# A hybrid decoder layer: the q, k, v units over the first token chunk alone, samples first, and the input norm's weight inside the hi/lo split

## The chip, the cores and the metric

The kernel is one program on one core of a Trainium2 chip. The metric is the device time of one execution in microseconds (us), as the median of several runs. Engines are named as in the profile: PE is TensorE's matmul stream and PEld its weight loads, DVE is VectorE, ACT is ScalarE, POOL is GpSimd, and SP (SyncE) issues most DMAs. Each engine works through its own instructions in order and waits on semaphores.

## The reference

One inference step of one layer, over 1024 prompt tokens and 8 samples of 4 tokens each (1056 tokens in all), model width 1024, everything in f32:

```
h = rmsnorm(x, g_mix_norm);  z = h @ w_in            # 2304 columns: q 512, k 128, v 128, B 512, C 512, h 512
q, k = rope(rmsnorm(q)), rope(rmsnorm(k))            # 8 q heads, 2 kv heads, width 64
o_attn = sliding-window (128) attention with a sink per head      # samples: over a cache of 128 keys
o_conv = B * conv3(C * h)                            # depthwise, causal
x = x + concat(rmsnorm(o_attn), rmsnorm(o_conv)) @ w_o
x = x + relu(rmsnorm(x) @ w_up)^2 @ w_down           # 4096 wide
x = x + sigmoid(rmsnorm(x) @ w_ple_gate) * (p @ w_ple)
```

## The kernel before, in words

The tokens lie on the free axis in three chunks of 352 (`CH`), the prompt first and the 32 sample tokens last. Every matrix product is made in three passes: each operand is split into a rounded part (`_hi`) and the rest (`_lo`), and PE multiplies hi by hi, lo by hi and hi by lo. For one unit of 128 output columns and one chunk that is a *fill*: 8 slices of the contraction times 3 passes, 24 matmuls of 128x352 into one of three `acc` banks (function `fill`). A fill needs its unit's weights split, which is ACT's `split_hi` and then `split_lo` on DVE or POOL, and then sends SP for the weights that take the freed slot; `w_st`, `w_hi` and `w_lo` have two slots each.

The input projection has 18 units, 54 fills with the index g: units 0 to 5 are q, k and v (`U_CONV` = 6), the others are C, h and B for four slices of the short convolution. Fill g is unit g // 3, chunk g % 3. A function `plan_inproj` gives the steps of attention that each engine does behind fill g (`at[g]`). For a tile t (0 the samples, 1 to 8 the prompt's blocks of 128) these are: B turns q, k, v to tokens on partitions (PE) and squares them; E norms and rotates (DVE, POOL's half of the sine term, ACT's and DVE's hi/lo split into `st_q`, `st_k`); S turns them back; Q makes the scores, DVE's masked maxima (`prob`), ACT's exponentials; D the denominators (POOL); P and R turn the probabilities; V and W multiply by v, ACT moves half of the result (`cross`), DVE adds and scales (`o_tok`); W also has ACT's square and POOL's root for the norm; N scales by it (ACT); O turns the result back. `plan_aux` hands these steps four of the five `aux` banks in turn, the fifth to V, W and O.

Ahead of the fills, x comes in 12 tiles of 88 rows: DVE squares (`x_sq`), POOL takes the root, ACT scales a copy (`x_nrm`), PE turns it, DVE multiplies by the norm's weight into `h_tmp`, ACT rounds (`act_hi`), POOL subtracts (`act_lo`). PE turns ten tiles (`ahead = 6` beyond the first four) before fill 0.

Behind fill 53 the output projection has 8 units of 3 fills (`out_units`). Each also turns a column slice of x (`x_col`, one buffer, loaded by SP once `x_turned` says that the last one was read) for the residual. A chunk of its input is ready when ACT and POOL have split attention's part (`mix_attention`, `lo_of_attention`) and DVE has normed the convolution's (`norm_conv`, `mix_conv`). The MLP and the embedding gate follow.

Of the kernel before, what the change touches and what calls it, by code (L numbers as in the profile page):

```python
# [25 lines left out]
P = 128  # L26
# [40 lines left out]
def plan_inproj():  # L67
# [44 lines left out]
def plan_aux(at):  # L112
# [3 lines left out]
    names = [("vec", 0, 0)]  # L116
    for g in range(3 * U_OUT):
        if g < NCH:
            names += [("x", g * XPC + t, h) for t in range(XPC) for h in range(2)]
        if g == NCH:  # L120
            names.append(("vec", 1, 0))
        if g > 3 * U_OUT - NCH:
# [17 lines left out]
def hybrid_step(nc, ins, outs):  # L140
# [49 lines left out]
    w_lo = place("w_lo", [P, 2, D], F32R)  # L190
    sq_sum = place("sq_sum", [P, NT], F32)
# [10 lines left out]
    kc = place("kc", [P, 4, DEC_B, WIN], F32R, conv_at)  # L202
    u_p = place("u_p", [P, SEQ + 2], F32)
# [4 lines left out]
    h_tmp = place("h_tmp", [P, 2, 4, XT], F32)  # L208
    root_c = place("root_c", [P, 2, CH], F32, cursor[0] - 4 * 2 * CH)
    x_at = cursor[0]  # L210
    tok = place("tok", [P, QK + KW], F32)
    ropea = place("ropea", [P, QK], F32)
    ropeb = place("ropeb", [P, QK], F32)
    st_q = place("st_q", [P, NQ, P], F32R)
    st_k = place("st_k", [P, 4, P], F32R)
    qt = place("qt", [P, NQ * P], F32R)
    kt = place("kt", [P, 2, 4 * P], F32R)
    v_parts = place("v_parts", [P, 3, NKV, 2, HD], F32R)
    x_end = cursor[0]
# [12 lines left out]
    columns = {"ms": NX, "rs": NX, "mse": NX, "mx": NQ, "nm": NQ, "sn": NQ, "es": NQ, "l": NQ, "den0": NQ, "den1": NQ,  # L232
# [1642 lines left out]
```

## Time and profile before

| | us |
|---|---|
| median of 3 runs (1413.68 to 1415.95) | 1413.86 |
| the profiled execution, first to last instruction (its span) | 1409.7 |
| of it, before the first fill of the input projection | 41.15 |
| fills 0 to 8 | 41.15 to 82.17 |
| fills 9 to 52 and most of attention | 82.17 to 388.61 |
| fill 53 and unit 0 of the output projection | 388.61 to 426.65 |
| units 1 to 7 of the output projection | 426.65 to 537.29 |
| the norm, MLP and gate, to the end | 537.29 to 1409.7 |

The times are ends of groups of matmuls in the trace. The profiled execution is known by its span; the runs' median lies 4.2 us above it, and times for the runs are worked out by carrying that distance along.

### The profile page before, as it was taken

Reading aid. Unit: us, or ns where it says so; the run is one execution under the profiler, and the core shown is the slowest. Engines: PE = TensorE matmul, PEld = TensorE weight load, DVE = VectorE, ACT = ScalarE, POOL = GpSimd, SP = SyncE. Lnnn points to the kernel's source line nnn. Section 1 sums busy time; section 2 is a strip of 40 time slices with the busy share of each in tenths; the row PEclk is TensorE's granted clock in tenths of the full one; section 3 lists DMA queues with packets and bytes.
Section 4 is the critical chain, followed back from the end, with each engine's and each line's share of the span. In section 5 each row is a group of like instructions: output and inputs, shape, how many; then the busy total and the mean of one; then the engine's idle time right before and its main releaser. Section 6 shows DMA issues by size and latency. Waiting matters only on the chain.

```text
span 1409.7 us, 21751 instructions
## 1 busy us (share of the span) xinstructions
PE 1315.8 (93%) x8348; PEld 1298.5 (92%) x8348; DVE 716.3 (51%) x1271; ACT 401.9 (29%) x801; POOL 199.2 (14%) x216
## 2 busy tenths in 40 slices
PE   3899988997958889999999999999999999999997
PEld 2899877897958889999999999999999999999997
DVE  6302757677575446435445344354453544587342
ACT  5332445455434222102111011121110211254232
POOL 6623434434130000000000000000000000041000
PEclk9999999999989899999999999999999999999999
DMA  5521011001103221321111111111111111111221
GB/s 153 131 60 32 1 48 30 16 16 35 46 17 75 62 65 41 77 52 45 48 47 54 45 45 45 45 45 45 45 45 45 45 50 39 46 45 54 69 68 46
DMA packets 111132, 70.99 MB, mean 50 GB/s; under 512 B 3226, under 2 KB 109622, under 8 KB 111064
## 3 DMA queue, kind: packets, MB, share of 16 engines
q1 hardware_dynamic: 110584, 68.37, 17.7%
q0 software_dynamic: 480, 1.93, 0.5%
q8 instruction: 33, 0.54, 0.2%
q14 instruction: 19, 0.16, 0.0%
q10 hardware_dynamic: 16, 0.00, 0.0%
HBM read 65.69 MB, written 5.54 MB: 51 GB/s over the span
## 4 chain that ended last, share of the span: by engine, by line
PE 77%; DVE 8%; ACT 4%; issue 4%; DMA 3%; POOL 2%; SPq 1%; DVEq 0%; ACTq 0%
PE acc L1534 71%; PE aux L1549 3%; DMA x_col<-in_x_sample 2%; DVE prob L1265 2%; PE aux L1534 1%; POOL act_lo L669 1%; DVE conv L1365 1%; POOL sq_sum L793 1%; DMA w_st<-in_w_in 1%; PE aux L1682 1%; DVE ropea L1218 1%; DVE o_tok L1305 1%; ACT sq_new L1097 1%; DVE pt_lo L1281 1%; ACT w_hi L805 0%
## 5 line engine op out<-in xcount | busy, mean ns | idle before, releaser
L1534 PE MATMUL acc<-xg_hi,w_hi 128*128 128x352 f32 x960 | 312.0, 325 | 0.0
L1534 PE MATMUL acc<-xg_lo,w_hi 128*128 128x352 f32 x960 | 307.8, 321 | 0.0
L1534 PE MATMUL acc<-xg_hi,w_lo 128*128 128x352 f32 x960 | 307.7, 321 | 0.0
L1534 PE MATMUL acc<-a_hi,w_hi 128*128 128x352 f32 x768 | 247.7, 323 | 0.0
L1534 PE MATMUL acc<-a_lo,w_hi 128*128 128x352 f32 x768 | 246.1, 320 | 0.0
L1534 PE MATMUL acc<-a_hi,w_lo 128*128 128x352 f32 x768 | 245.9, 320 | 0.0
L1534 PE MATMUL acc<-act_hi,w_hi 128*128 128x352 f32 x624 | 215.1, 345 | 13.2 <-issue 12.8
L1534 PE MATMUL acc<-act_hi,w_lo 128*128 128x352 f32 x624 | 208.3, 334 | 0.0
L1534 PE MATMUL acc<-act_lo,w_hi 128*128 128x352 f32 x624 | 208.2, 334 | 0.0
L1449 DVE TENSOR_TENSOR xt<-acc,xt 128x352 f32<-128x352 f32 x192 | 100.3, 522 | 179.1 <-PE acc L1534 178.1
L805 ACT ACTIVATE w_hi<-w_st 128x1024 fp32r<-128x1024 f32 x98 | 102.9, 1050 | 280.0 <-PE acc L1534 273.8
L1534 PEld LDWEIGHTS acc<-xg_lo,w_hi 128*128 128x128 f32 x960 | 180.5, 188 | 0.2
L1534 PEld LDWEIGHTS acc<-xg_hi,w_hi 128*128 128x128 f32 x960 | 180.1, 188 | 0.3 <-issue 0.2
L1534 PEld LDWEIGHTS acc<-xg_hi,w_lo 128*128 128x128 f32 x960 | 180.0, 188 | 0.0
L1534 PEld LDWEIGHTS acc<-a_lo,w_hi 128*128 128x128 f32 x768 | 144.3, 188 | 0.0
L1534 PEld LDWEIGHTS acc<-a_hi,w_hi 128*128 128x128 f32 x768 | 144.1, 188 | 0.0
L1534 PEld LDWEIGHTS acc<-a_hi,w_lo 128*128 128x128 f32 x768 | 143.9, 187 | 0.0
L793 POOL TENSOR_TENSOR sq_sum<-sq_sum,sq_new 128x352 f32<-128x352 f32 x24 | 23.2, 966 | 837.8 <-ACT sq_new L1097 837.8
L1534 PEld LDWEIGHTS acc<-act_hi,w_hi 128*128 128x128 f32 x624 | 124.8, 200 | 14.2 <-issue 13.2
L1068 ACT ACTIVATE a_hi<-relu 128x352 fp32r<-128x352 f32 x96 | 47.9, 499 | 292.6 <-DVE relu L1432 292.6
L1432 DVE SCALAR_TENSOR_TENSOR relu<-acc,rstd 128x352 f32<-128x352 f32 x96 | 50.3, 524 | 154.5 <-PE acc L1534 154.5
L1534 PEld LDWEIGHTS acc<-act_lo,w_hi 128*128 128x128 f32 x624 | 124.7, 200 | 0.0
(199 smaller groups left out, 1598.6 us busy)
## 6 DMA issues: line engine op xcount, KB each, us to landing
w_st<-in_w_up SPq DMA_DIRECT2D x32, 512.0 KB, 4.1
w_st<-in_w_down SPq DMA_DIRECT2D x32, 512.0 KB, 3.4
w_st<-in_w_in SPq DMA_DIRECT2D x18, 512.0 KB, 3.9
w_st<-in_w_o SPq DMA_DIRECT2D x8, 512.0 KB, 4.6
w_st<-in_w_ple_gate SPq DMA_DIRECT2D x8, 512.0 KB, 4.3
x_nat<-in_x_prompt SPq DMA_DIRECT2D x11, 352.0 KB
x_col<-in_x_prompt SPq DMA_DIRECT2D x8, 484.0 KB
out<-y_col SPq DMA_DIRECT2D x8, 484.0 KB
```

The costliest lines, as they stand in the source:

```text
L669: pool.tensor_tensor(act_lo[:, 4 * h:4 * h + 4, cols], h_tmp[:, h, :, :], act_hi[:, 4 * h:4 * h + 4, cols], ALU.subtract).then_inc(h_lo, 1)
L793: pool.tensor_tensor(sq_sum[:, chunk(c)], sq_sum[:, chunk(c)], sq_new[:, :], ALU.add)\
L805: act.activation(w_hi[:, s, :], w_st[:, s, :], ACT.Copy).then_inc(whi_ready, 1)
L1068: act.activation(a_hi[:, m, chunk(c)], relu[:, f % 2, :], ACT.Square).then_inc(a_hi_ready, 1)
L1097: act.activation(sq_new[:, :], xt[:, 2 * m + n2, chunk(c)], ACT.Square).then_inc(squared, 1)
L1218: dve.tensor_tensor(heads(ropea, m), qn, cos[:, None, :].broadcast_to([m, NQ + NKV, HD]), ALU.mult).then_inc(cos_ready, 1)
L1265: e = dve.tensor_tensor_reduce(prob[:, h * 2 * P:(h + 1) * 2 * P] .rearrange("p (s k) -> p s k", s=2), bank[:, cols].rearrange("p (s k) -> ...
L1281: frees(dve.tensor_tensor(pt_lo[0:rows_, cols], bank[0:rows_, 0:width], pt_hi[0:rows_, cols], ALU.subtract), step, t, i)
L1432: dve.scalar_tensor_tensor(out=relu[:, f % 2, :], in0=acc[c][:, 0:CH], scalar=0.0, in1=rstd[:, chunk(c)], op0=ALU.max, op1=ALU.mult)\
L1449: dve.tensor_tensor(xt[:, n, chunk(c)], acc[f % 3][:, 0:CH], xt[:, n, chunk(c)], ALU.add)\
L1534: ins_ = pe.matmul(out, w[a][cols], x[b][tile_], start=(k == 0 and p == 0), stop=(k == len(terms) - 1 and p == 2))
L1549: ins_ = pe.transpose(out[dst], src, ident[0:src.shape[0], 0:src.shape[0]])
```

## The change

It leaves every matmul of the products as it is and orders the first stage anew.

- Tokens are numbered with the samples first. `plan_fills` lists the 54 fills: units 0 to 5 over chunk 0; then units 4 and 5 over chunks 1 and 2, while their weights still stand; then units 0 to 3 over chunks 1 and 2, for which four weight blocks are loaded a second time (`EXTRA` = 4); then the other units as before. `LAST_FILL` decides when a slot's next weights are split. DVE makes the lo part of loads 0 to 6, POOL of the rest.
- x is scaled in its own buffer and turned by chunk, 4 tiles of one slice of 128 columns at a time. ACT writes the hi part from the turned bank with the norm's weight as its scale, and DVE writes the lo part from the bank by one multiply-subtract. `h_tmp`, DVE's multiplication and POOL's subtraction go.
- The x tiles of chunks 1 and 2 are normed and turned behind fills 0 to 7 (`X_NORM_AT`, `X_TURN_AT`).
- Attention begins behind fill 7 and not 18. Tiles start at fills 7, 11, 14, 18, 22 and so on by four (before: 18, 22 and so on by three), in the order 1, 2, 0, 3 to 8. N and O come one fill later than before.
- Some tables, `smask`, the cached keys and values have other places and load times; the rotary table comes tile by tile from POOL.
- A unit of the output projection turns all three chunks of its x slice ahead of its first fill.

The core of the diff:

```diff
+ORDER = [1, 2, 0, 3, 4, 5, 6, 7, 8]
+POS = {t: n for n, t in enumerate(ORDER)}
...
+    fills = [(u, 0, u) for u in range(U_CONV)]
+    fills += [(u, c, u) for c in (1, 2) for u in (4, 5)]
+    fills += [(u, c, U_CONV + u) for u in range(4) for c in (1, 2)]
+    fills += [(u, c, u + EXTRA) for u in range(U_CONV, U_OUT) for c in range(NCH)]
...
+EXTRA = 4
+FILLS = plan_fills()
+LAST_FILL = {load: g for g, (u, c, load) in enumerate(FILLS)}
...
+SPLIT_AT = {g: [n + 2 for n in LAST_FILL if LAST_FILL[n] == g] for g in range(3 * U_OUT)}
+
+X_NORM_AT = {0: [4], 1: [5], 2: [6], 3: [7], 4: [8], 5: [9, 10], 6: [11]}
+X_SQUARE_AT = {-1: [4], 0: [5], 1: [6], 2: [7], 3: [8], 4: [9, 10], 5: [11]}
+X_TURN_AT = {3: [(1, k) for k in range(4)], 4: [(1, k) for k in range(4, 8)],
+             6: [(2, k) for k in range(4)], 7: [(2, k) for k in range(4, 8)]}
+AHEAD = 4
...
-        at[3 + b].append(("k", b))
-        at[4 + b].append(("K", b))
-    at[12].append(("C", 0))
-    starts = [18, 22, 25, 28, 31, 34, 37, 40, 43]
-    for t, g in enumerate(starts):
+        at[CACHE_AT + b // 2].append(("k", b))
+        at[CACHE_AT + 1 + b // 2].append(("K", b))
+    at[CACHE_AT].append(("C", 0))
+    starts = [7, 11, 14, 18, 22, 26, 30, 34, 38]
+    for t, g in zip(ORDER, starts):
         late = 1 if t == 0 else 0
         for step, off in (("B", 0), ("E", 1), ("S", 3), ("Q", 4), ("D", 4), ("P", 6), ("V", 7), ("R", 7), ("W", 8),
-                          ("N", 9 + late), ("O", 9 + late)):
+                          ("N", 10 + late), ("O", 10 + late)):
             at[g + off].append((step, t))
...
             for t in range(XPC):
                 load_x(t)
-            load_w(0, in_unit(0), None)
-            for t in range(XPC, 2 * XPC):
-                load_x(t)
-            load_w(1, in_unit(1), None)
-            for t in range(2 * XPC, NX):
+            load(0)
+            load(1)
+            load_x(4)
+            load(2)
+            load_x(5)
+            load_x(6)
+            load(3)
+            load_x(7)
+            load(4)
+            filled(sp, "x", 0, KT - 1)
+            load_x(8)
+            load(5)
+            for t in range(9, NX):
                 load_x(t)
...
+            def norm_x(t):
+                act.wait_ge(x_rs, t + 1)
+                act.activation(x_tile(t)[0:XT, :], x_tile(t)[0:XT, :], ACT.Copy,
+                               scale=stat["xrs"][0:XT, t:t + 1]).then_inc(x_normed, 1)
+
+            def hi_of_x(c, k):
...
+                bank = filled(act, "x", c, k)
+                act.activation(act_hi[:, k, chunk(c)], bank[:, 0:CH], ACT.Copy,
+                               scale=vec[:, V_MIX + k:V_MIX + k + 1]).then_inc(h_hi, 1)
...
+            def lo_of_h(c, k):
+                bank = filled(dve, "x", c, k)
+                dve.wait_ge(h_hi, KT * c + k + 1)
+                frees(dve.scalar_tensor_tensor(out=act_lo[:, k, chunk(c)], in0=bank[:, 0:CH],
+                                               scalar=vec[:, V_MIX + k:V_MIX + k + 1], in1=act_hi[:, k, chunk(c)],
+                                               op0=ALU.mult, op1=ALU.subtract), "x", c, k)
...
+            for g, (u, c, n) in enumerate(FILLS):
+                if g == FIRST_FILL[n]:
+                    pe.wait_ge(wlo_ready, n + 1)
+                if g >= NACC:
+                    pe.wait_ge(acc_free[g % NACC], g // NACC)
+                fresh = g in (0, U_CONV, U_CONV + 2)
+                fill(c, n % 2, act_in, g % NACC, lo_of_h_ready(c) if fresh else None)
...
+                for c_, k in X_TURN_AT.get(g, []):
+                    turn_x(c_, k)
...
             def out_units(i, first):
                 for s in range(2):
-                    pe.wait_ge(wlo_ready, 2 * i + (U_OUT + s + 1))
                     pe.wait_ge(xcol_landed, 96 * i + 48 * (s + 1))
                     for c in range(NCH):
                         pe.wait_ge(aux_free[c], 2 * i + (OUT_USE[c] + s))
                         turn(aux[c], [((every, slice(k * XT, (k + 1) * XT)), x_col[0:XT, XPC * c + k, :])
                                       for k in range(XPC)]).then_inc(x_turned, 1)
+                    pe.wait_ge(wlo_ready, 2 * i + (W_OUT + s + 1))
+                    for c in range(NCH):
                         pe.wait_ge(att_lo, c + 1)
                         pe.wait_ge(mix_lo, c + 1)
```

Three places show how instructions stand on an engine. The first is the start of PE's stream; `aux<-ident,x_nrm` is a turn of x. Before:

```order
L1549 MATMUL aux<-ident,vec_nat 128x8
L1549 MATMUL aux<-ident,x_nrm 128x88 x80
L1534 MATMUL acc<-act_hi,w_hi 128x352
L1534 MATMUL acc<-act_lo,w_hi 128x352
L1534 MATMUL acc<-act_hi,w_lo 128x352
```

and of the change:

```order
L1633 MATMUL aux<-ident,vec_nat 128x8
L1633 MATMUL aux<-ident,x_nat_94 128x88 x20
L1618 MATMUL acc<-act_hi,w_hi 128x352
L1618 MATMUL acc<-act_lo,w_hi 128x352
L1618 MATMUL acc<-act_hi,w_lo 128x352
L1633 MATMUL aux<-ident,x_nat_94 128x88 x4
L1618 MATMUL acc<-act_hi,w_hi 128x352
```

The first fill moved from behind 80 turns (ten tiles) to behind 20, and the rest of its chunk's turns went in between its matmuls.

The second is ACT in the middle of attention, from the exponentials of one tile (`prob`) on; `st_q`, `st_k` are step E of the next tile, `cross` and `aux,stats<-o_tok` step W, `o_tok<-o_tok` step N, `pt_hi` step P. Before:

```order
L913 ACTIVATE prob,stats<-prob,stats 128x256 x8
L918 ACTIVATE stats<-stats 128x8
L878 ACTIVATE st_q<-ropea 128x8x64
L880 ACTIVATE st_k<-ropea 128x256
L805 ACTIVATE w_hi<-w_st 128x1024
L935 ACTIVATE cross<-aux 128x256
L943 ACTIVATE aux,stats<-o_tok 128x512
L888 ACTIVATE v_parts<-tok 128x2x64
L895 ACTIVATE qt<-aux 128x512 x2
L900 ACTIVATE kt<-aux 128x512
```

and of the change:

```order
L978 ACTIVATE prob,stats<-prob,stats 128x256 x8
L983 ACTIVATE stats<-stats 128x8
L1000 ACTIVATE cross<-aux 128x256
L1008 ACTIVATE aux,stats<-o_tok 128x512
L943 ACTIVATE st_q<-ropea 128x8x64
L945 ACTIVATE st_k<-ropea 128x256
L871 ACTIVATE w_hi<-w_st 128x1024
L1080 ACTIVATE conv<-u_p,vec 128x1024
L1081 ACTIVATE conv<-u_s,vec 128x32
L1012 ACTIVATE o_tok<-o_tok,stats 128x512
L992 ACTIVATE pt_hi<-aux 128x512 x2
```

Step W moved ahead of step E, and the copies of step S (`qt`, `kt`) moved behind N and P.

The third is PE at the start of the output projection. Before:

```order
L1549 MATMUL aux<-ident,tail 18x128 x4
L1549 MATMUL aux<-ident,x_col 128x88 x4
L1534 MATMUL acc<-act_hi,w_hi 128x352
...
L1534 MATMUL acc<-act_hi,w_lo 128x352
L1695 MATMUL aux<-sq_sum,ones 128x352
L1549 MATMUL aux<-ident,x_col 128x88 x4
```

and of the change:

```order
L1633 MATMUL aux<-ident,tail 18x128 x4
L1633 MATMUL aux<-ident,x_col 128x88 x12
L1618 MATMUL acc<-act_hi,w_hi 128x352
```

The turns of chunks 1 and 2 moved from between the fills to ahead of them.

## Rows read from the trace of the kernel before

**Rows 1.** Busy time by stretch: PE, PEld, DVE, ACT, POOL, granted clock, DMA share, GB/s.
```profile
0.00:41.15 41.15, 14.04 (x81) 11.85 (x82) 29.02 (x42) 21.52 (x30) 26.73 (x37) 1.00 0.62 160
41.15:82.17 41.02, 40.54 (x253) 39.97 (x253) 8.51 (x15) 14.92 (x30) 20.36 (x30) 1.00 0.37 96
82.17:388.61 306.44, 277.47 (x1850) 269.87 (x1849) 178.33 (x387) 139.87 (x364) 115.03 (x115) 0.96 0.11 31
388.61:426.65 38.04, 22.92 (x127) 21.26 (x126) 30.26 (x38) 15.08 (x22) 13.84 (x11) 0.87 0.12 30
426.65:537.29 110.64, 96.47 (x588) 94.52 (x587) 50.76 (x93) 35.21 (x72) 0.00 (x0) 0.92 0.27 63
```

**Rows 2.** Waits of PE from 82.17 to 388.61: total, times, longest us.
```profile
PE aux L1549 <- ACT qt L895: 21.6, 7, 6.3
```

**Rows 3.** Timeline of the opening: start, us, DVE, ACT, POOL and PE.
```profile
11.56 1.21 DVE L1150 CUSTOM_DVE_ANT_0 x_sq<-x_nat 88x1024 f32<-88x1024 f32 x1
14.99 1.22 DVE L501 TENSOR_TENSOR w_lo<-w_st,w_hi 128x1024 fp32r<-128x1024 f32 x1
19.41 2.83 DVE L1150 CUSTOM_DVE_ANT_0 x_sq<-x_nat 88x1024 f32<-88x1024 f32 x1
12.77 1.06 ACT L805 ACTIVATE w_hi<-w_st 128x1024 fp32r<-128x1024 f32 x1 [0.59 <-DMA w_st<-in_w_in]
13.73 1.13 ACT L826 ACTIVATE x_nrm<-x_nat,stats 88x1024 f32<-88x1024 f32 x1
51.86 1.00 ACT L982 ACTIVATE qkv<-acc 128x352 f32<-128x352 f32 x2
14.41 0.55 POOL L657 TENSOR_TENSOR stats<-stats,half 88x1 f32<-88x1 f32 x1
40.00 1.44 PE L1549 MATMUL aux<-ident,x_nrm 88*128 88x88 f32 x8 [3.33 <-ACT x_nrm L826]
```

**Rows 4.** Page, costliest groups: xcount, then busy us, mean ns.
```profile
L1432 DVE SCALAR_TENSOR_TENSOR relu<-acc,rstd 128x352 f32<-128x352 f32 x96 | 50.3, 524 | 154.5 <-PE acc L1534 154.5
```

**Rows 5.** Groups by form, 218.43 to 349.96 (five tiles): busy us, mean ns.
```profile
L913 ACT ACTIVATE prob<-prob,stats 128x256 f32<-128x256 f32 x40 | 19.8, 496 | 15.1 <-DVE stats L1273 15.1
L1297 DVE TENSOR_TENSOR o_tok<-aux,cross 128x256 f32<-128x256 f32 x10 | 4.2, 422 | 11.3 <-PE aux L1549 7.4 <-ACT cross L935 3.9
L943 ACT ACTIVATE aux<-o_tok 128x512 f32<-128x512 f32 x5 | 3.0, 602 | 16.1 <-DVE o_tok L1305 16.1
L465 POOL TENSOR_TENSOR tok<-ropeb,rope_p 128x320 f32<-128x320 f32 x5 | 5.9, 1171 | 1.0 <-DVE ropeb L1212 0.9
L1222 DVE TENSOR_TENSOR ropea<-ropea,tok 128x640 f32<-128x640 f32 x5 | 4.1, 824 | 0.2
L878 ACT ACTIVATE st_q<-ropea 128x512 fp32r<-128x512 f32 x5 | 3.2, 634 | 6.0 <-DVE ropea L1222 6.0
L947 ACT ACTIVATE o_tok<-o_tok,stats 128x512 f32<-128x512 f32 x5 | 3.7, 731 | 0.0
L501 POOL TENSOR_TENSOR w_lo<-w_st,w_hi 128x1024 fp32r<-128x1024 f32 x5 | 13.0, 2600 | 8.4 <-ACT w_hi L805 8.4
```

**Rows 6.** Timeline of DVE around fill 53.
```profile
393.57 4.38 DVE L1320 SCALAR_TENSOR_TENSOR conv<-conv,vec,root_c 128x352 f32<-128x352 f32 x4
397.88 0.68 DVE L1309 TENSOR_TENSOR qkv<-aux,vec 128x512 f32<-128x512 f32 x1
406.81 2.65 DVE L1320 SCALAR_TENSOR_TENSOR conv<-conv,vec,root_c 128x352 f32<-128x352 f32 x4
```

**Rows 7.** The chain of work that ended last: start, us, what.
```profile
453.00 5.05 DMA x_col<-in_x_sample
458.69 5.43 PE acc L1534 x24
464.43 3.86 PE acc L1534 x24
...
540.02 641.01 PE acc L1534 x4032
```

More of the change, by code:

```diff
@@ L313, in hybrid_step @@
         tables_landed = sem("tables_landed")
+        rope_landed = [sem(f"rope_landed{s}") for s in range(2)]
         smask_landed = sem("smask_landed")
@@ L482, in pt_count, with exp_count @@
         def pt_count(t, step):
-            before = 0 if t == 0 else 6 + 4 * (t - 1)
+            before = sum(6 if x == 0 else 4 for x in ORDER[:POS[t]])
             return before + (0 if step == "P" else 3 if t == 0 else 2)
+        def exp_count(t):
+            return sum(NKV if x == 0 else NQ for x in ORDER[:POS[t]])
         def gains(at_, n, m):
@@ L923, in consume @@
                             filled(act, "V", t, "o")
-                        if i == 0 and step == "P" and t:
-                            filled(act, "W", t - 1, "o")
+                        if i == 0 and step == "P" and pos:
+                            filled(act, "W", before, "o")
                         rows_, width = (P, 4 * P) if i < 2 else (NS, P)
@@ L1153, in gain_h @@
-            def gain_h(t):
-                for h in range(2):
-                    bank = filled(dve, "x", t, h)
-                    if t >= 1:
-                        dve.wait_ge(h_lo, 2 * t - 1 + h)
-                    frees(dve.tensor_tensor(h_tmp[:, h, :, :], bank[:, 0:4 * XT].rearrange("p (k t) -> p k t", k=4),
-                                            gains(V_MIX + 4 * h, 4, XT), ALU.mult), "x", t, h)
+                dve.tensor_tensor_reduce(x_sq[0:XT, :], x_tile(t)[0:XT, :], x_tile(t)[0:XT, :], 1.0 / D, EPS,
+                                         ALU.mult, ALU.add, stat["xms"][0:XT, t:t + 1]).then_inc(x_ms, 1)
@@ L1173, in _ @@
                     split_lo(dve, 1, 2)
-            bank = filled(dve, "vec", 1, 0)
-            frees(dve.tensor_copy(vec[:, V_MLP:NV], bank[:, V_MLP:NV]), "vec", 1, 0)
-            done_with(dve, "vec", 1, 0)
+            for t in X_SQUARE_AT[-1]:
+                ms_of_x(t)
             def consume(step, t):
-                m = rows_of(t)
+                m, pos = rows_of(t), POS[t]
+                before = ORDER[pos - 1] if pos else None
                 w = NKV if t == 0 else NQ
@@ L1332, in _ @@
                 u, c = divmod(g, NCH)
+                for n in SPLIT_AT[g]:
+                    if n < DVE_SPLITS:
+                        split_lo(dve, n % 2, n + 1)
+                if g == VEC_AT:
+                    bank = filled(dve, "vec", 1, 0)
+                    frees(dve.tensor_copy(vec[:, V_MLP:NV], bank[:, V_MLP:NV]), "vec", 1, 0)
+                    done_with(dve, "vec", 1, 0)
+                for t in X_SQUARE_AT.get(g, []):
+                    ms_of_x(t)
+                for c_, k in X_TURN_AT.get(g, []):
+                    lo_of_h(c_, k)
                 if u >= U_CONV:
@@ L1528, in take_bank, with product @@
                 return aux[bank]
-            def product(out, w, x, terms, more=False):
+            def product(out, w, x, terms, before=None):
                 for k, (cols, tile_) in enumerate(terms):
+                    if before is not None:
+                        before(k)
                     for p, (a, b) in enumerate(((0, 0), (0, 1), (1, 0))):
```

529 lines of the change are left out of this document (273 added, 256 removed).

## The prediction

> **What bounds the kernel now.** I first read the busy time by stretch [rows 1]. PE is busy 14.04 of the first 41.15 us, 40.54 of the next 41.02, 277.47 of 306.44, 22.92 of 38.04 and 96.47 of 110.64; behind 540.02 the chain of waits is one piece of PE work, 641 us long [rows 7]. So PE sets the end, and what a change of order can win is the time for which PE stands still in the first 537 us: 27.1 us ahead of the first fill, 29.0 beside attention, 15.1 around fill 53, 14.2 in the output projection, and what a lower clock costs there (granted 0.87 and 0.92, against 1.00 at the start). The waits of PE name whom it waits for: of the 29.0 beside attention 21.6 are ACT's copy `qt`, seven times, the longest 6.3 [rows 2]. That is the end of a tile's way through E (DVE, POOL, ACT) and S (PE), for which before leaves two fills. In the output projection the chain goes through the load of `x_col`, 5.05 us, behind which the next fill takes 5.43 and the one after it 3.86 [rows 7].
>
> A fill is 3.86 us at full clock; with its split weights present and its banks free it has no other cost.
>
> **The opening.** Before the change PE turns ten x tiles and then begins. Each tile goes through a square (1.21 us, but 2.83 beside POOL), a root (0.55), the scaled copy (1.13) and PE's turns, 0.72 for four [rows 3]. With the change only four tiles stand ahead. 160 GB/s flowed in the first stretch [rows 1], and the weights' hi part begins at 12.77 [rows 3], when the same first tiles and weights have landed; so the fourth tile's copy is done by about 14.5, the hi part of its first bank at 15.6, two lo splits on DVE (1.22 and, for the bank, about 0.5) at 17.4. **The first fill starts at 17.5 and not at 41.15.** In it lie the turns of slices 4 to 7, which ACT and DVE answer in turn at about 0.5 each (ACT copies a chunk from a bank in 0.50 [rows 3]; for DVE's new multiply-subtract see below): it ends near 24. Fills 1 to 3 follow at 3.86 and end at 35.6. Then PE wants chunk 1 turned, and its last tile's norm waits in ACT's row behind a weight split (1.06) and two unit copies: 3.3 us, then eight banks at 0.35 to 0.5. Fill 4 ends at 44.3; fill 5, behind the rest of chunk 1, at 49.7; fill 6 at 53.5; the last tile of chunk 2 costs 1.6 more, and with the turns of chunk 2 and step B of the first tile fill 7 ends near 62.5 and **fill 8 at 66.8**, for 82.17 before: 15.4 won. Of the 23.6 won at the first fill, 8 go back to turns and norms that formerly lay ahead of it.
>
> The *new operation*, a multiply-subtract out of a PSUM bank, 24 times, has no row. Its nearest is DVE's relu, which has the same operands and size: 0.524 [rows 4], 12.6 us in all. From below nothing excludes that it hides wholly (it stands ahead of PE at fill 0 and at chunk changes only); from above, the square beside POOL shows a factor of 2.83/1.21 = 2.3 [rows 3], which would make it 29 us, of which a third, chunk 0's, is bare: +5. I take 0.52, as the POOL subtraction that stood beside it is gone. The Trainium skill (GPSIMD Engine Reference, section "8. Key points") says that GpSimd and VectorE share their way into SBUF and collide when VectorE runs in a two-port mode or reads two operands from SBUF. By that rule the new operation, with one operand in PSUM, is not slowed, and the sum stays as it is; by the squares' row taken for all operations it would be the 5 us more. No row shows this operation.
>
> **Fills 9 to 52 and attention.** PE's work in this stretch was 277.5 [rows 1]. Turns of the cached keys that before lay ahead of it come in (+2.1), step B of tile 1 goes out (0.85), step O of tile 8 comes in ahead of fill 53 (0.66): 279.4. Its waits I work out tile by tile. A tile now has four fills for a period and not three. Time is counted from the end of the fill behind which B stands. PE does B, Q and W (5.0), two fills and P (1.15) and comes to step O at 13.9. The row that must be through by then: the exponentials, eight at 0.50, end at 8.7, since the first wait for ACT's copies and DVE's square, sum and first maximum; then `cross` and two times DVE's addition 0.42 with its multiplication (10.15), ACT's square 0.60 and its read-out (11.0), POOL's root (12.0), and POOL's sine term of the *next* tile, 1.17 (13.2), DVE's addition 0.82 (14.05), ACT's `st_q` 0.63 with `st_k` (15.05) and only then step N, 0.73: 15.75 [rows 5]. W was moved ahead of E, but N stands behind E on ACT. **PE waits 1.85 in an undisturbed tile**, and this wait takes the place of the one for `qt`, which now has a fill more. Where POOL's weight split, 2.60 [rows 5], gets ahead of the sine term, up to 2.6 is added: the slot's last fill stands behind E of tiles 4 and 7 (fills 23 and 35), and a little later at fills 26 and 38 (1.5 to 2.5 for 5 and 8). Tile 4 also meets the samples' result on its way through memory (`o_moved`), for which ACT's row waits. So my waits are 9.1 for tiles 1, 2 and 0 together (the split parts of k, Q and S of the first tiles, which have no period to fill), 2.2 for tile 3, 7.1, 4.4, 1.85, 5.2 and 3.4 for tiles 4 to 8: **33.3, no less than the 29.0 of before**. Fill 52 ends at 66.8 + 279.4 + 33.3 = 379.5, for 388.61: **of 15.4, 9.1 are left.** The bounds: nothing of these waits, when N falls in time, and twice as much.
>
> **The tail.** At fill 53 DVE's four scalings of the convolution take 4.38 beside POOL's and step O's work, later 2.65, and step O takes 0.68 of DVE between them [rows 6]. Tile 8 is through long before, so both go: 1.73 + 0.68 = **2.4** (bounds 0 and 4). The chunks stay bound by DVE's and ACT's norm.
>
> **The output projection.** Its last seven units take 110.64 [rows 1], 15.8 each. Turned ahead, the slice frees `x_col` at the start of a unit, and its 5.05 us load [rows 7] has three fills, 11.6 us, to hide in; what follows at full clock is 3 fills of 3.86 and 12 turns, at half of the 0.18 that one took cold [rows 3] 1.0: 12.6 x 7 = 88.2. **22.4 won** (bounds 14 and 24: at the busy time with its slow stretches, 96.5 [rows 1], it would be only 14).
>
> The rest is untouched: four more loads keep the slots' order. The four loads themselves are hidden by fills 10 to 17, each 512 KB with two fills for it. **Sum: 9.1 + 2.4 + 22.4 = 33.9 off a span of 1409.7, 1375.8. The runs' median was 4.2 above the span, so 1380.**
>
> **The rivals.** *Four fills are enough.* If the split of a tile's work is less serial than I laid it (maxima and exponentials faster, POOL out of the way), PE waits 2 us and not 33.3: 1380 - 31 = 1349. For it: the waits of before have one name, `qt`, and the change gives just that one a third fill. Against it: N behind E, worked out above.
>
> *The loads pace the opening.* Fills 0 to 5 each need a new unit, with the x tiles of chunks 1 and 2 on the same queues. At the 160 GB/s of [rows 1] four units and five tiles (3.9 MB) take some 24 us, and the six fills with the turns 26 to 32. With little less bandwidth, or with slots freed too late (ACT's and DVE's splits stand behind norms), each fill waits one to two us: +7, 1387. By the Trainium skill (DMA: Bandwidth & Descriptors, section Specifications, Bandwidth) a core gets about 358 GB/s from HBM; by an estimate from that figure the first tiles and weights would land some 5 us earlier and the time would be about 1375. The rows of this kernel's own start, 160 GB/s, do not agree, and they decide.
>
> *The hoisted turn does not do what it says.* If the load's cost is not the wait but the slow fill behind it, or the load is late again (its issue stands behind other issues on SP), the 22.4 stay: 1402.
>
> *The other side.* Step order on ACT can turn the wait for N into a chain that is longer than four fills, so that every tile is late by the same amount. The gains, 33.9 with the waits at 33.3, are gone when the nine tiles wait 67.2 us, 7.5 each; beyond that it is slower; at 9 each, 81 us, the time would be 1380 + 48 = 1428. The longest wait before was 6.3 [rows 2], and the period has grown by a fill; little speaks for it.
>
> **How the numbers follow.** Forecast, 1366 to 1392: 0.50. Four fills enough, about 1349: 0.25. Loads pace the opening, about 1387: 0.14. Hoist without effect, about 1402: 0.05. The other side: 0.05, and 0.01 for the neighbourhood of no change. The first three hold 0.89; with some room for their edges the range is 1346 to 1398: from the waits all gone, and 3 us more, to the waits half as large again, or loads and new operation at their upper bounds. A measurement of this kernel can tell about 0.2% from no change, 2.8 us. Faster 0.93, the same 0.02, slower 0.05.
>
> **What would show it.** First fill at 17.5, with DVE's lo parts at 0.52 each; the end of fill 8 near 67, with no PE wait for a weight split; fill 52 at 379; PE waits of about 33 us between them, the most of them in step O for ACT's `o_tok` and behind it in S for `st_q`; output units 12.6 us apart, without `x_col` on the chain and with a clock near 1.00. Wrong it is if waits for weights or x stand in the first six fills, if PE's waits are far from 33, or if the units remain near 15.8.

## The result, and the profile after

The changed kernel takes 1406.85 us (median of 4, 1405.78 to 1407.92); the kernel before took 1414.9 beside it. The ratio is 0.9946, 95% interval 0.9927 to 0.9965: faster by 0.5%, some 8 us, where 34 were forecast. The profiled execution spans 1406.1 us, and the median lies 0.7 above it (4.2 before). In e8 and in e12 below one execution ran far slower than the others (1521.4 and 2699.3 us); their medians are those of the others.

Busy time of the changed kernel by stretch, cut at the same events as [rows 1] (first fill, fill 8, fill 52, unit 0 and unit 7 of the output projection; columns as there):

```profile
0.00:18.34 18.34, 3.39 (x22) 3.09 (x22) 7.52 (x13) 9.63 (x12) 5.69 (x19) 1.00 0.69 161
18.34:71.25 52.91, 48.36 (x302) 47.18 (x302) 28.50 (x46) 27.03 (x43) 10.57 (x22) 0.90 0.58 146
71.25:408.43 337.18, 290.19 (x1863) 283.00 (x1862) 176.43 (x395) 145.51 (x375) 117.29 (x125) 0.90 0.12 34
408.43:446.37 37.94, 24.86 (x121) 23.07 (x122) 29.46 (x33) 14.79 (x21) 12.88 (x10) 0.78 0.12 30
446.37:533.17 86.80, 86.80 (x589) 86.67 (x588) 50.59 (x92) 34.34 (x71) 0.00 (x0) 1.00 0.34 80
```

| stretch, us | before | after | moved | forecast |
|---|---|---|---|---|
| to the end of fill 8 | 82.17 | 71.25 | -10.9 | -15.4 |
| fills 9 to 52, attention | 306.44 | 337.18 | +30.7 | +6.3 |
| fill 53, unit 0 of the output projection | 38.04 | 37.94 | -0.1 | -2.4 |
| units 1 to 7 | 110.64 | 86.80 | -23.8 | -22.4 |

The rest, to the end, takes 872.93 for 872.41. So one of the four terms came about as worked out (units 1 to 7), the opening brought some 70% of what was forecast, the tail nothing, and attention's stretch swallowed it all: it has 47.0 us of PE standing still (337.18 less 290.19) for 29.0, and 12.7 more of PE busy, at a granted clock of 0.90 for 0.96. PE's waits in it (total, times, longest), where [rows 2] had `qt`:

```profile
PE aux L1633 <- ACT o_tok L1012: 29.5, 8, 8.2
PE aux L1677 <- DVE st_k L1299: 8.3, 2, 4.3
PE aux L1657 <- DVE k_parts L1255: 2.6, 1, 2.6
...
PE aux L1633 <- ACT qt L960: 1.3, 1, 1.3
```

The wait for `qt` is gone and one for `o_tok` (step N) stands in its place, larger. ACT's timeline shows why, here in a period in which PE stood ready for step O of tile 4 from 269.84 to 276.00 (`prob` is tile 5, `st_q` and `st_k` are tile 6; start, us):

```profile
265.42 0.49 ACT L978 ACTIVATE prob<-prob,stats 128x256 f32<-128x256 f32 x1
...
267.39 0.60 ACT L1008 ACTIVATE aux<-o_tok 128x512 f32<-128x512 f32 x1 [1.02 <-DVE o_tok L1376]
...
271.51 0.63 ACT L943 ACTIVATE st_q<-ropea 128x512 fp32r<-128x512 f32 x1 [3.40 <-DVE ropea L1293]
272.04 0.40 ACT L945 ACTIVATE st_k<-ropea 128x256 fp32r<-128x256 f32 x1
272.35 1.04 ACT L871 ACTIVATE w_hi<-w_st 128x1024 fp32r<-128x1024 f32 x1
273.97 1.15 ACT L1080 ACTIVATE conv<-u_p,vec 128x1024 f32<-128x1024 f32 x1 [0.58 <-DVE u_p L1429]
275.03 0.31 ACT L1081 ACTIVATE conv<-u_s,vec 128x32 f32<-128x32 f32 x1
275.24 0.71 ACT L1012 ACTIVATE o_tok<-o_tok,stats 128x512 f32<-128x512 f32 x1
```

The square of this tile was done at 268; then ACT waits 3.40 for the rotation of the tile two on, splits it, and before it comes to N (L1012) it makes a weight's hi part and the first tap of the convolution (1.04, a wait of 0.58, 1.15 and 0.31): 2.8 us from the end of `st_k` to the start of N that have nothing to do with this tile.

That is so for O of this tile alone. For O of tiles 3, 5 and 6 PE waits 6.37, 8.15 and 4.73, but 0 to 0.7 us of other work stand between `st_k` and N on ACT; the rotation itself comes later, and a weight's lo part on POOL is ahead of it. The rows ahead of O of tile 5, and then of tile 6:

```profile
304.35 2.58 POOL L552 TENSOR_TENSOR w_lo<-w_st,w_hi 128x1024 fp32r<-128x1024 f32 x1
304.66 2.96 DVE L1289 TENSOR_TENSOR ropea<-ropeb,rope_p 128x640 f32<-128x640 f32 x1
306.90 1.43 POOL L512 TENSOR_TENSOR tok<-ropeb,rope_p 128x320 f32<-128x320 f32 x1
309.29 0.63 ACT L943 ACTIVATE st_q<-ropea 128x512 fp32r<-128x512 f32 x1 [6.07 <-DVE ropea L1293]
```

```profile
326.86 2.38 POOL L552 TENSOR_TENSOR w_lo<-w_st,w_hi 128x1024 fp32r<-128x1024 f32 x1 [14.78 <-ACT w_hi L871]
327.92 2.00 DVE L1270 TENSOR_TENSOR ropea<-tok 128x640 f32<-128x640 f32 x1 [4.38 <-ACT tok L937]
342.32 0.63 ACT L943 ACTIVATE st_q<-ropea 128x512 fp32r<-128x512 f32 x1 [3.46 <-DVE ropea L1293]
343.16 0.71 ACT L1012 ACTIVATE o_tok<-o_tok,stats 128x512 f32<-128x512 f32 x1
```

Ahead of O of tile 5 the split stands before POOL's sine term (`tok`), and DVE's cosine product (L1289) takes 2.96 beside it, for 0.81 in the period of tile 4. Ahead of O of tiles 6 and 3 it stands early in the period, where DVE's square of q and k (L1270) takes 2.00 and 2.35 beside it, for 0.83.

The output projection looks as forecast; its chain has no load in it any more, where [rows 7] had one a unit:

```profile
446.37 0.91 PE aux L1633 x12
447.28 11.49 PE acc L1618 x72
458.77 0.91 PE aux L1633 x12
459.68 11.49 PE acc L1618 x72
```

### The profile page after: what moved, and what is told of

Read it like the earlier page. It is cut to its first block, busy times and chain, and to the rows that moved or that the text cites. A ratio compares the mean times of both kernels' runs of the same rounds, so it can differ in the third digit from the quotient of the medians.

```text
span 1406.1 us, 21754 instructions
## 1 busy us (share of the span) xinstructions
PE 1318.2 (94%) x8348; PEld 1304.3 (93%) x8348; DVE 711.9 (51%) x1276; ACT 406.8 (29%) x805; POOL 169.6 (12%) x197
## 4 chain that ended last, share of the span: by engine, by line
PE 77%; ACT 5%; DVE 4%; issue 3%; POOL 2%; SPq 0%; DMA 0%; ACTq 0%; DVEq 0%; POOLq 0%
PE acc L1618 70%; PE aux L1633 3%; PE aux L1758 2%; ACT prob L978 2%; PE aux L1618 1%; POOL sq_sum L859 1%; PE aux L1677 1%; DVE prob L1336 1%; ACT sq_new L1170 1%; ACT w_hi L871 0%; POOL tok L512 0%; ACT o_tok L1012 0%; DVE ropea L1293 0%; DVE ropea L1270 0%; DVE w_lo L552 0%
## 5 line engine op out<-in xcount | busy, mean ns | idle before, releaser
L871 ACT ACTIVATE w_hi<-w_st 128x1024 fp32r<-128x1024 f32 x102 | 107.3, 1052 | 324.2 <-PE acc L1618 322.4
L1141 ACT ACTIVATE a_hi<-relu 128x352 fp32r<-128x352 f32 x96 | 47.9, 499 | 292.5 <-DVE relu L1514 292.5
L552 DVE TENSOR_TENSOR w_lo<-w_st,w_hi 128x1024 fp32r<-128x1024 f32 x86 | 105.4, 1225 | 50.1 <-ACT w_hi L871 49.8
```

The costliest lines, as they stand in the source:

```text
L552: eng.tensor_tensor(w_lo[:, s, :], w_st[:, s, :], w_hi[:, s, :], ALU.subtract).then_inc(wlo_ready, 1)
L871: act.activation(w_hi[:, s, :], w_st[:, s, :], ACT.Copy).then_inc(whi_ready, 1)
L1141: act.activation(a_hi[:, m, chunk(c)], relu[:, f % 2, :], ACT.Square).then_inc(a_hi_ready, 1)
```

## The experiments

Two theories stood at first. **Place:** step N stands behind too much on ACT, and the wait that this makes costs twice, itself and in the clock behind it. **Length:** a tile's work on DVE and POOL is simply too long for its fills, whatever the order. "Stretch" below is the time from the end of fill 8 to the end of fill 52 in the profiled run of each: 306.4 before, 337.2 after. It shows more than the median does, since the opening's end wanders: in the profiles of the changed kernel and of e2 to e5 and e7 to e9, which leave the opening as it is, fill 8 ends between 64.8 and 71.4.

**e1, the hoisted turns alone, on the kernel before.**

```diff
 def out_units(i, first):
     for s in range(2):
-        pe.wait_ge(wlo_ready, 2 * i + (U_OUT + s + 1))
         pe.wait_ge(xcol_landed, 96 * i + 48 * (s + 1))
         for c in range(NCH):
             ...
+        pe.wait_ge(wlo_ready, 2 * i + (U_OUT + s + 1))
+        for c in range(NCH):
             pe.wait_ge(att_lo, c + 1)
```

> The kernel before with one part of the change alone: a unit of the output projection turns its three chunks of x ahead of its first fill. Theory: this part is separable and is worth what the changed kernel's trace shows in that stretch, units 1 to 7 in 87 us for 110.6, so about 1391 us (1414.9 less 24), granted clock 1.00 there. Rival: the gain there is owed to something else in the change (other load order, earlier release of SP), and then the time stays within 5 us of 1414.9.

1391.72 us (ratio 0.9846, 0.9812 to 0.9881). Units 1 to 7, columns as above:

```profile
427.44:514.22 86.78, 86.78 (x590) 86.66 (x588) 50.29 (x92) 34.12 (x70) 0.00 (x0) 1.00 0.34 80
```

The theory holds to the microsecond. It also says something about the rest of the change: this one move gives 22 us beside its own runs of the kernel before (1413.88), the whole change 8. **All else in it together cost 14 to 15 us.**

**e2, step N a fill earlier.**

```diff
-                          ("N", 10 + late), ("O", 10 + late)):
+                          ("N", 9 + late), ("O", 10 + late)):
```

> The changed kernel with one number altered: step N one fill earlier, so that ACT scales o_tok ahead of the next tile's st_q and st_k, the weight's hi part and the convolution's first tap, all of which stand ahead of it in the changed kernel. Theory (ACT's row): PE's waits for o_tok fall from 29.5 us to 5 or less, fills after them take 4.1 and not 5.4 to 6.3, and the time is 1375 to 1382. Rival (POOL and DVE: root, sine and weight split are late whatever ACT's order): N still waits for the root, PE's waits for o_tok stay above 20, time 1400 or more. A second rival: the wait moves on to S (st_k), time 1390 to 1400.

1391.69 us (0.9836, 0.9800 to 0.9872), 15 less than the changed kernel; stretch 323.3 for 337.2. PE's waits:

```profile
PE aux L1677 <- DVE st_k L1299: 12.1, 3, 4.4
PE aux L1633 <- ACT o_tok L1012: 5.4, 4, 2.6
```

The waits for `o_tok` fell from 29.5 to 5.4, as *place* says, but the time fell only to the value of the second rival: `st_k` rose from 8.3 to 12.1, and the clock stayed at 0.90. Place explains 14 of the 31 us lost. Seventeen are left, and the line of the stretch shows where:

```profile
71.37:394.67 323.30, 292.51 (x1863) 285.26 (x1862) 176.29 (x395) 146.66 (x375) 117.55 (x125) 0.90 0.12 35
```

PE stands still for 30.8 us in it, nearly as before the change (29.0), but is busy for 292.5 and not 277.5. What is left is work at the low clock, not waiting; and it did not shrink with the 16 us of waits that e2 took away.

**e3, e8, matmuls in the place of a wait.** They compute nothing that is needed. e3 puts 20 ahead of O in the changed kernel; e8 puts 22 ahead of S in tiles 2, 4 and 7 of e2 (the diff is e8's).

```diff
 if step == "S":
+    if t in (2, 4, 7):
+        bank = take_bank("S", t, "q0")
+        for _ in range(22):
+            pe.matmul(bank[:, 0:CH], ident_r[:, :], act_hi[:, 0, chunk(0)], start=True, stop=True)
     pe.wait_ge(st_lo, 2 * (pos + 1))
```

> The changed kernel with 20 matmuls of 128x352 that compute nothing needed put ahead of PE's wait for o_tok in step O of tiles 3 to 7; they overwrite a bank that the turn overwrites again. Theory (part of the loss is PE's clock after a wait): the waits shrink by what the matmuls take, 3.2 us each, the fills behind them fall from 5.4 to 6.3 to about 4.1, and the time falls by 6 to 9 us, to 1398 to 1401. Rival (the fills behind a wait are slow for another cause, such as banks or weights not free): they stay slow, the time is the same or some us longer, where the wait was shorter than the matmuls.

e3: 1406.83 us (0.9961, 0.9942 to 0.9979): no gain in time, so the expected 6 to 9 us did not come. In its profile the stretch is 333.5, 3.7 less, with 17 us of added matmuls in it (100 at 0.17), 13.9 us less waiting and a clock of 0.93: some of the low clock went, not enough to be seen in the median. (The profiled execution took 1400.57 us, the quickest of the ten.)

> The kernel with N a fill earlier (1391.7), and 22 matmuls of 128x352 that compute nothing needed put ahead of PE's wait for st_k in step S of tiles 2, 4 and 7, where it waited 3.9, 4.4 and 3.8 us; they write a bank that S overwrites. Theory (the granted clock of 0.50 to 0.60 that follows such a wait costs as much as the wait): the waits fall under 1 us, the stretches behind them run at 1.00, and 3 to 4 us a place are won, 1380 to 1384. Rival (the clock is low there for another cause): the stretches behind stay at 0.5 to 0.6, time 1391 to 1393.

e8: 1386.41 us (0.9817, 0.9778 to 0.9856), 5 less than e2 and not 8 to 11, and not clear of noise, as the intervals overlap. The stretch is 316.1 for 323.3, but the profiled execution is e8's quickest (1381.8) and e2's slowest (1394.33). The places differ. Twelve us behind the wait of tile 2, in e2 and then in e8:

```profile
114.73:120.73 6.00, 6.00 (x29) 5.68 (x29) 2.94 (x5) 4.13 (x10) 4.45 (x4) 0.50 0.31 90
120.73:126.73 6.00, 6.00 (x32) 6.00 (x32) 2.68 (x6) 1.58 (x3) 3.23 (x4) 0.69 0.00 0
```

```profile
111.10:117.10 6.00, 5.56 (x46) 5.24 (x47) 3.71 (x7) 4.97 (x13) 5.25 (x5) 1.00 0.31 89
117.10:123.10 6.00, 6.00 (x46) 6.00 (x45) 3.56 (x13) 1.75 (x3) 3.82 (x4) 1.00 0.00 1
```

In the same 12 us PE does 61 instructions at 0.50 and 0.69, and 92 at 1.00. Behind tile 4's S, where three smaller waits (0.83, 1.74 and 1.49 us) follow the filled one, the clock fell all the same, to 0.63 and 0.52. Behind tile 7's S, where only waits of 0.29 and 0.45 us are left, it stood at 0.74 and 0.69, for 0.50 and 0.67 in e2. So at one place of three the clock stayed up when the wait was filled; that filling a wait always buys it back is not shown.

**e4, e6, two small places in the opening and the tail.** e4 puts the turns of the first output unit back between its fills; e6 turns chunk 1 of x one fill later.

```diff
-X_TURN_AT = {3: [(1, k) for k in range(4)], 4: [(1, k) for k in range(4, 8)],
+X_TURN_AT = {4: [(1, k) for k in range(4)], 5: [(1, k) for k in range(4, 8)],
```

> The changed kernel with the turns of x of the first unit of the output projection put back between its fills; units 1 to 7 as changed. Theory (the hoisted turn of the first unit waits for ACT's copies at 420.5 and 422.2 and holds fill 54 back): fill 54 starts 1 us earlier, the sum for the norm of the last chunk and with it the last fill of the unit 1 to 2 us earlier, 1405. Rival (chunk 0's fill is bound by DVE's lo part, ready at 421.6): nothing, 1406.8, within 0.5.

e4: 1406.85 us (0.9948, 0.9929 to 0.9967). Fill 54 starts 13.3 us behind fill 52's end and not 14.4, as the theory has it, but unit 0 ends 37.6 behind it for 37.9: the fill was late and cost nothing. The rival holds.

> The changed kernel with the turns of chunk 1 of x one fill later (behind fills 4 and 5, not 3 and 4). Theory: PE's wait of 2.6 us for the norm of x tile 7 and the slow fill behind it (5.97 for 4.0) go, about 1 us is given back ahead of fill 6, whose operand comes later; fill 8 ends 3 to 4 us sooner, time 1403. Rival (the opening's end is set by the last x tile, which has its own chain): fill 8 ends where it did, 1406.8.

e6: 1405.29 us (0.9937, 0.9916 to 0.9958). The wait of 2.6 for x's norm is gone, fill 4 starts at 36.4 and not 41.5, fill 8 ends at 64.9; but so early it also ended in e7, where the opening was not touched. The stretch behind it, whose steps are the changed kernel's, took 341.0 for 337.2, with the same waits (47.1 for 47.0) and 3.7 us more of busy PE, which hides most of what the opening won. Not settled by this run; e10 tries it again.

**e7, POOL relieved of the weights (on e2).**

```diff
-DVE_SPLITS = 7
+DVE_SPLITS = 23
```

> The kernel with N a fill earlier (1391.7), and DVE making the lo part of all the input projection's weights, where POOL made it from load 7 on. Theory (POOL's weight split, 2.4 us, ahead of the sine term makes PE's remaining waits in S for st_k): the waits of 4.4 and 3.8 us in tiles 4 and 7 shrink by 1.5 to 2.5 each, with the clock behind them: 1384 to 1388. Rival (DVE's own row is now the late one; 1.23 us more per load on it, and 16 loads): the waits stay or grow, 1392 to 1398.

1402.52 us (0.9913, 0.9885 to 0.9942), 11 more than e2; stretch 328.2 for 323.3, in a profile of the quickest of the five runs (1392.95, the next 1400.3). The waits for `st_k` in tiles 4 and 7 grew to 5.5 and 4.7. The rival holds in its direction, with a time above its range: POOL's splits of 2.6 us, to which the prediction had charged part of these waits, were the cheaper place.

**e5, e9, e10, the spacing of the tiles.** e5 starts tiles 4 to 8 every three fills; e9 has N and O nine fills behind as well, so that attention is spaced as before; e10 is e9 with the edit of e6.

```diff
-    starts = [7, 11, 14, 18, 22, 26, 30, 34, 38]
+    starts = [7, 11, 14, 18, 21, 24, 27, 30, 33]
...
-                          ("N", 10 + late), ("O", 10 + late)):
+                          ("N", 9 + late), ("O", 9 + late)):
```

> The changed kernel with tiles 4 to 8 started every three fills (21, 24, 27, 30, 33) and not every four; nothing else altered. Then step E of a tile stands ahead of W and N of the one two before it, as in the kernel before. Theory (it is the place of N behind E on ACT that makes the wait, not the number of fills): PE's waits for o_tok fall under 6 us, waits for qt or st_k of 2 to 6 us a tile come back, and the sum of the waits is 30 to 40; time 1392 to 1404. Rival (a tile needs its four fills): the waits grow, 1412 or more.

e5: 1403.95 us (0.9918, 0.9890 to 0.9946), at the upper end of the theory's range; stretch 336.0. Waits for `o_tok` are 3.1 us in all, for `qt` 17.3, and a new one came, 10.1 us in V for DVE's `qkv`: O now stands directly ahead of V, which wants O's bank back. A fourth fill was not what the tiles needed, and the third alone did not help.

> The changed kernel with the steps of attention spaced as before the change: tiles 4 to 8 every three fills, steps N and O one fill earlier, so that O stands ahead of a fill and not ahead of V. The opening, the fill order and the hoisted turns stay as changed. Theory (the spacing of the steps, not their early start, loses what the opening wins): fills 9 to 52 take 306 to 315 us where the changed kernel took 337 and before 306; with fill 8's end 65 to 71 the time is 1376 to 1388, faster than the changed kernel and than the kernel before with the hoist alone (1391.7). Rival (the early start itself is dear: the cached keys, the samples and the first tiles now stand beside x's last tiles and loads): 325 or more for these fills, time 1395 or more.

e9: 1393.95 us (0.9862, 0.9844 to 0.9879); stretch 323.9. Between the two theories, nearer to the rival: spaced as before, the same work took 17 us longer than before. Its largest waits in sum are again those of before, for `qt`; the longest single one is 6.84, for `o_tok` of tile 1:

```profile
PE aux L1633 <- ACT qt L960: 17.8, 5, 5.0
```

> The same with the turns of chunk 1 of x one fill later as well. Theory: the 2.6 us wait and, where it came, the slow fill go from the opening, 2 to 4 us less than the run beside it: 1373 to 1385. Rival (the opening's end is set by the last x tile): no difference that five rounds can tell, under 2 us.

e10: 1388.41 us (0.9816, 0.9801 to 0.9831), 5.5 less than e9 beside it: the later turn of chunk 1 pays, somewhat more than expected. Stretch 325.4. The profiles settle what e6 left open: with the later turn fill 8 ends at 63.2 to 64.9 in six of them (e6, e10 to e14), without it at 64.8 to 71.4 in eight, 69.0 in the mean.

**e11 to e14, where attention begins.** All on e10. e11 takes the start and the tile order of before; e13 keeps the order and alters the starts alone; e12 moves step O of tile 1 by a fill; e14 leaves tiles 1, 2 and 0 early and moves the others by one fill. (In e11, e13 and e14 POOL waits once for DVE's last weight split, which keeps the two in order; up to fill 14, behind that wait, e14 runs within 0.1 us of e10.)

```diff
-ORDER = [1, 2, 0, 3, 4, 5, 6, 7, 8]
+ORDER = [0, 1, 2, 3, 4, 5, 6, 7, 8]                   # e11
-    starts = [7, 11, 14, 18, 21, 24, 27, 30, 33]
+    starts = [18, 22, 25, 28, 31, 34, 37, 40, 43]       # e11
+    starts = [12, 15, 18, 22, 25, 28, 31, 34, 37]       # e13
+    starts = [7, 11, 14, 19, 22, 25, 28, 31, 34]        # e14
-                          ("N", 9 + late), ("O", 9 + late)):
+                          ("N", 9 + late), ("O", 9 + late + (t == 1))):   # e12
```

> The opening, the fill order, the hoisted turns and the later turn of chunk 1 (as in the run with 1388.4), but attention as before the change in all that spaces it: samples first, starts at fills 18, 22, 25, 28 and so on by three, N and O nine behind. POOL waits once for DVE's last weight split before its own first. Theory (an early start is itself dear: tiles 1, 2 and 0 wait 16 us in all and lower the clock, where fills 9 to 17 ran without a wait before): fills 9 to 52 take 306 to 312 us and the time is 1370 to 1378. Rival (the loss lies in what else was moved, the key turns, the rotary table tile by tile, the buffers): 318 to 326 again, 1384 to 1392.

e11: 1369.66 us (0.9670, 0.9644 to 0.9695), stretch 307.2; the stretch is in the theory's range, the time 0.3 below it. It is 37 us faster than the changed kernel.

> The run with 1388.4 (three fills a tile, N and O nine behind, turns of chunk 1 later), with step O of tile 1 alone one fill later. Theory (PE's longest wait there, 6.85 us for tile 1's o_tok at fill 16, is one of place only): the wait and the low clock behind it go, 7 to 10 us, 1378 to 1382. Rival (it moves on to the samples' S or to P of tile 2 right behind): within 3 us of 1388.4.

e12: 1383.99 us (0.9787, 0.9765 to 0.9809), 4 less than e10 and not 7 to 10. The wait of 6.85 is gone, one of 2.7 for `qt` came nearby; the stretch is 322.0.

> As the run with 1388.4, with the tiles' order of the change kept (1, 2, 0, 3 to 8) but all starts some five fills later: 12, 15, 18, 22, 25, 28, 31, 34, 37. Theory (the early start is dear because tile 1 and 2 stand where x's last tiles, the cached keys and the second loads of the weights are worked on): the wait of 6.85 us goes and with it part of the others; fills 9 to 52 take 307 to 315 us, 1370 to 1378. Rival (the order, with the samples third, is dear wherever it starts): 318 or more, 1381 or more.

e13: 1370.19 us (0.9683, 0.9660 to 0.9707), stretch 308.2: the start, not the order of the tiles. But it moved two things, the early three tiles and, by some fills, the place of the others in their units; e14 parts them. And *length* falls: at three fills a tile, e11 and e13 take within 2 us of what the kernel before took.

> As the run with 1388.4, tiles 1, 2 and 0 started at 7, 11 and 14 as in the changed kernel, but tiles 3 to 8 at 19, 22, 25, 28, 31 and 34, on the second fill of a unit as in the run with 1370.2 and not on its first. Theory (the early first three tiles are what is dear): fills 9 to 52 take 318 or more, 1381 or more. Rival (it is the place of tiles 3 to 8 within their units, against the convolution's and the weights' work): 308 to 314, 1371 to 1377.

e14: 1376.93 us (0.9727, 0.9704 to 0.9750), stretch 312.0. **The rival holds:** with tiles 1, 2 and 0 as early as in the changed kernel, one fill's shift of the six others gives 13 of the 17 us. The stretches of e10, e14 and e13:

```profile
64.71:390.12 325.41, 286.71 (x1863) 277.56 (x1862) 181.16 (x395) 145.50 (x375) 117.87 (x124) 0.92 0.12 35
```

```profile
64.22:376.19 311.97, 279.99 (x1862) 271.34 (x1862) 178.01 (x395) 145.92 (x375) 116.91 (x124) 0.95 0.13 37
```

```profile
63.22:371.45 308.23, 279.70 (x1869) 270.94 (x1868) 186.57 (x397) 146.42 (x377) 120.90 (x127) 0.96 0.13 37
```

The shift takes 6.7 us of waits (38.7 to 32.0) and 6.7 us of slow PE (286.7 to 280.0). What it moves is seen in DVE's row between step E (`st_k`) of tile 5 and step W (`o_tok`) of tile 3, e10 and then e14:

```profile
222.33 1.17 DVE L1299 TENSOR_TENSOR st_k<-ropea,st_k 128x256 fp32r<-128x256 f32 x1
223.42 3.31 DVE L1447 SCALAR_TENSOR_TENSOR conv<-u_p,vec,conv 128x352 f32<-128x352 f32 x2
226.84 0.53 DVE L1454 TENSOR_TENSOR conv<-acc,conv 128x352 f32<-128x352 f32 x1
227.28 0.42 DVE L1368 TENSOR_TENSOR o_tok<-aux,cross 128x256 f32<-128x256 f32 x1
```

```profile
224.87 1.18 DVE L1301 TENSOR_TENSOR st_k<-ropea,st_k 128x256 fp32r<-128x256 f32 x1
225.97 0.41 DVE L1370 TENSOR_TENSOR o_tok<-aux,cross 128x256 f32<-128x256 f32 x1
```

And ACT in e10, which stands in W, waits for that `o_tok`, and has `qt` of tile 5 behind it:

```profile
228.19 0.60 ACT L1008 ACTIVATE aux<-o_tok 128x512 f32<-128x512 f32 x1 [4.89 <-DVE o_tok L1376]
...
229.79 1.08 ACT L960 ACTIVATE qt<-aux 128x512 fp32r<-128x512 f32 x2
```

In e10 two taps of the convolution (3.31 us beside POOL's weight split; the same pair takes 1.19 in the changed kernel's tail, with POOL idle) and its last product fall between E and W; in e14 nothing stands there. Followed through e10, the same 3.8 us stand there in one other tile, and these two have the longest of its waits for `qt`, 4.96 us each; where 0.6 and 2.2 us of other work stand there, PE waits 1.55 and 1.97. In e14 no tile has the 3.8, and the waits for `qt` are 0.65 to 2.27. The kernel before has them in two tiles as well (3.7 us, waits of 4.04 and 3.67), so the shift wins something that was open there too. What tiles 1 and 2 wait at their early start (2.60, 1.23, 3.93 and 6.84 us in e10) stands in e14 as it did.

## Why the prediction was wrong

**The step that failed is the account of fills 9 to 52**, "the row that must be through by then", which put N at 15.75 and PE's wait at 1.85 in an undisturbed tile, and 33.3 in all. By the spans the miss is 30.3 us (1406.1 for 1375.8), and 24.5 of it lie here: 47.0 us of waits for 33.3, and 290.2 of PE's work for 279.4. The opening adds 4.5 and the tail 2.3, the output projection gives back 1.4; the medians differ by less, 26.9, since the median lay 0.7 and not 4.2 above the span, which is luck. The mechanism was named rightly (W ahead of E, N behind E, so that the wait for `qt` gives way to one for N). Three things in its sum were not right:

- *The row ahead of N was not counted whole.* The table below sets PE's waits beside the forecast, by the tile whose B and E stand in the period, as the prediction counts them: what is too small begins with tile 5. The 1.85 is the undisturbed tile, the period shown above (E of tile 6, N of tile 4). There N ends 19.1 us after the fill ahead of B and not 15.75, and 2.8 of the 3.3 are `w_hi` and the convolution's first tap. They stood in the rows of the order, between `st_k` and `o_tok`, and the sum passed over them. In the periods of tiles 5, 7 and 8 (N of tiles 3, 5 and 6) N ends at 19.5, 21.0 and 18.2; there the sum had POOL's weight split, but not DVE's slower steps beside it. And PE came to step O at 12.9 to 13.6 and not at 13.9. e2, which takes N out from behind all this, shows the size: 14 us of the stretch.
- *PE's work was summed at the old clock.* 279.4 was forecast, 290.2 came, at 0.90. Each of the longer waits was followed by slow work, such as fills of 4.8 to 6.3 us for 4.06 (5.80 and 6.09 behind the waits of 6.37 and 6.15). The size does not go by the sum of the waits: e2 and e14 wait 30.8 and 32.0 us, and PE is busy for 292.5 and 280.0; what sets it stays open. The prediction read this very price in the output projection and did not carry it to the waits that it forecast.
- *The place of a tile against the units was not in the sum.* A period of four fills against units of three puts E and W of every tile beside other pieces of the convolution. e10, e13 and e14 show 13 us for a shift of a single fill, at a period of three; how much of the changed kernel's loss it makes at four was not measured by itself.

| PE's waits, us | tiles 1, 2, 0 | 3 | 4 | 5 | 6 | 7 | 8 | behind |
|---|---|---|---|---|---|---|---|---|
| forecast | 9.1 | 2.2 | 7.1 | 4.4 | 1.85 | 5.2 | 3.4 | 0 |
| measured (over 0.3) | 9.6 | 2.5 | 7.1 | 6.4 | 6.15 | 8.15 | 5.2 | 1.2 |

What e2 did not win back, 16.9 us against before, is 15.0 of busy PE (1.9 of them forecast as new work) and 1.8 of waits, so nearly all of it is the second of these. How much of that comes from the third, at a period of four, stays open.

*The opening*: the step was right, the size off. First fill at 18.34 (17.5 forecast), fill 8 at 71.25 (66.8); eight profiles with the same opening spread over 64.8 to 71.4, by a first fill at 16.5 to 18.4 and by fills 4 and 7, which took 4.1 to 6.2 us behind their waits. The forecast of 66.8 lies within that spread, so most of the miss here is chance. No wait for a weight's lo part came; the rival of the loads did not show. The new multiply-subtract took 0.574 to 0.585 in all 24, for 0.52 taken; the factor of 2.3 did not apply to it. The Trainium skill (GPSIMD Engine Reference, section "8. Key points") names, beside a two-port mode of VectorE, two operands in SBUF as what collides with GpSimd. The traces agree with this, as the taps show, which read two from SBUF (3.31 beside POOL, 1.19 alone); POOL was little busy beside the new operation, 10.6 of 52.9 us, so its own case is not fully tried.

*The tail*: right that step O left DVE's row there (0.68), wrong that the contention would: DVE's four scalings took 3.74, 2.62 and 3.75 in the three chunks, for 4.38 and 2.65 in the first two before [rows 6], since POOL's lo part of attention stands beside the first and the third. -0.1 for -2.4.

*The output projection*: -23.8 for -22.4, by the mechanism named; e1 shows it alone.

*The rivals*: that the change would not do what it says, and that four fills are enough, did not happen; "the other side" was held at 0.05 with 67 us of waits as its point. 47 us of waits and 11 of slow clock came near it, the waits by the order on ACT that it names, the clock by a way that was not priced.

## What to carry to other kernels

When a step is moved on an in-order engine, write down every instruction that now stands between its operand and it, those of other work too, and add their times: the step that the change moved is rarely the only thing that moved. Look at the clock behind a PE wait as well as at the wait, and read both from a trace: here the sum of the waits did not tell the slow work. Check the period of a pipeline against the period of the work that it runs beside; one fill's shift was worth 13 us here. Take a change apart before judging it: a small part, twelve turns hoisted, held more than the whole gain, and with attention begun later the rest was good as well (1369.7 for 1414.6).

## What the runs showed of the hardware

Of the granted clock, in places where PE had been waiting: in e2 it was 0.50, the lower of its two levels (1.2 of 2.4 GHz), for the 6 us behind a wait of 3.9, and 0.69 on average in the 6 us after them; in e8, where matmuls stood in the wait's place, it was 1.00. And behind the waits of the opening, which is alike in eight of the kernels, it was granted differently from run to run; with the first fill's start this moved the end of fill 8 by up to 6.6 us. Fills 9 to 52 wander too: they took 337.2, 337.1 and 341.0 in the changed kernel, e4 and e6, which leave them alike, the last with the same waits and a clock of 0.89 for 0.90.

At the start the granted clock of the profile does not fit the matmuls. In the changed kernel it reads 1.00 from 18.34 to 21.8 us, but there those of 128x352 start 0.29 us apart, as they do later at 0.50 (59.4 to 62.6); behind 21.8 it is 0.16.

Beside POOL's lo part of a weight, steps of DVE that read two operands in SBUF took 2 to 4 times as long: 2.96 for 0.81, 2.00 and 2.35 for 0.83, 3.31 for 1.19 us. The multiply-subtract out of PSUM took 0.574 to 0.585 in all 24.
